# The token sums of a seven-product MLP block on VectorE instead of GpSimd

## What is computed

```python
h = _rmsnorm(x, g_pre_mlp)
f = jnp.square(jax.nn.relu(h @ w_up)) @ w_down
return x + _rmsnorm(f, g_post_mlp)
```

## Time and profile before

| | |
|---|---|
| time, median of 3 runs | 1090.42 us (1085.86 to 1091.12) |
| profiled execution | 1090.3 us |
| its span in the trace | 1088.7 us, 20822 instructions |
| mean granted clock of TensorE | 0.991 |
| busy: TensorE | 1051.5 us (97%) |
| busy: VectorE, ScalarE, GpSimd | 638.2, 482.1, 231.9 us |

### The profile page before, as it was taken

How to read it: one execution, slowest core, us unless ns; L and a number is a source line. 1 busy time by engine, 2 the same in 40 slices (tenths; PEclk the granted TensorE clock), 3 DMA queues, 4 the chain that set the end, 5 groups by cost and what they waited for, 6 DMA issues and landing times.

```text
span 1088.7 us, 20822 instructions
## 1 busy us (share of the span) xinstructions
PE 1051.5 (97%) x7528; PEld 896.3 (82%) x7528; DVE 638.2 (59%) x1229; ACT 482.1 (44%) x1026; POOL 231.9 (21%) x290
## 2 busy tenths in 40 slices
PE   7999999999999999999999999999899999999997
PEld 6987877887778777777779987998699889889985
DVE  5244535444765665555554847349877458447756
ACT  5253223323554465555543446344246236424641
POOL 4003111321001023333332000106642034024200
PEclk9999999999999999999999999999899999999999
DMA  6522214234125789999965261122332333333322
GB/s 204 142 82 59 60 56 137 61 83 139 40 58 161 247 286 343 335 332 335 336 206 183 82 227 39 59 79 78 89 104 90 100 95 88 116 112 98 110 87 87
DMA packets 114416, 153.16 MB, mean 141 GB/s; under 512 B 9597, under 2 KB 66434, under 8 KB 114322
## 3 DMA queue, kind: packets, MB, share of 16 engines
q1 hardware_dynamic: 99808, 106.98, 32.1%
q0 software_dynamic: 13120, 44.08, 12.2%
q10 hardware_dynamic: 1394, 0.83, 0.3%
HBM read 144.76 MB, written 7.10 MB: 139 GB/s over the span
## 4 chain that ended last, share of the span: by engine, by line
PE 82%; DVE 7%; DMA 3%; issue 3%; ACT 2%; SPq 1%; POOLq 1%; POOL 0%; DVEq 0%; ACTq 0%
PE ps L475 29%; PE ps L2661 12%; PE ps L910 7%; PE ps L510 7%; PE ps L483 5%; PE ps L1944 4%; PE ps L926 3%; PE ps L448 2%; DMA kring<-in_cache_k_dram 2%; PE ps L1953 2%; PE ps L1985 2%; PE ps L1074 1%; DVE xn L565 1%; PE ps L1094 1%; PE ps L1969 1%
## 5 line engine op out<-in xcount | busy, mean ns | idle before, releaser
L360 DVE TENSOR_TENSOR w<-w,w 128x512 fp32r<-128x512 f32 (+1 forms) x192 | 154.9, 818 | 159.0 <-ACT w L349 153.8
L349 ACT ACTIVATE w<-w 128x512 fp32r<-128x512 f32 (+1 forms) x192 | 115.1, 609 | 209.5 <-PE ps L483 148.4
L475 PE MATMUL ps<-w,hid 128*128 128x512 f32 x672 | 163.9, 393 | 5.0 <-DVE wide L2904 5.0
L475 PEld LDWEIGHTS ps<-w,hid 128*128 128x128 f32 x672 | 127.5, 190 | 32.0 <-issue 5.4
L475 PE MATMUL ps<-w,hT 128*128 128x512 f32 x576 | 146.1, 403 | 1.9 <-ACT ri L831 1.9
L475 PEld LDWEIGHTS ps<-w,hT 128*128 128x128 f32 x576 | 106.5, 191 | 27.1 <-issue 5.3
L910 PE MATMUL ps<-hT,w 128*128 128x288 f32 x768 | 126.8, 307 | 0.0
L910 PEld LDWEIGHTS ps<-hT,w 128*128 128x128 f32 x768 | 105.0, 188 | 12.3 <-issue 11.6
L1911 POOL DMA_DIRECT2D vring<-in_cache_v_dram x128 | 69.1, 539 | 172.2 <-issue 172.2
L2115 DVE COPY kT<-ps 128x512 f32<-128x512 f32 x64 | 44.1, 689 | 74.8 <-PE ps L1944 74.6
L1944 PEld LDWEIGHTS ps<-ident,kring 128*128 128x128 f32 x512 | 56.6, 141 | 37.5 <-DMA kring<-in_cache_k_dram 21.3
(11 more groups left out here) (403 smaller groups left out, 1811.2 us busy)
## 6 DMA issues: line engine op xcount, KB each, us to landing
kring<-in_cache_k_dram SPq DMA_DIRECT2D x128, 256.0 KB, 4.1
vring<-in_cache_v_dram POOLq DMA_DIRECT2D x128, 256.0 KB, 4.5
w<-in_w_in_dram SPq DMA_DIRECT2D x88, 256.0 KB, 2.9
w<-in_w_down_dram SPq DMA_DIRECT2D x64, 256.0 KB, 2.9
w<-in_w_up_dram SPq DMA_DIRECT2D x40, 256.0 KB, 2.9
b<-in_w_up_dram SPq DMA_DIRECT2D x36, 256.0 KB, 4.0
w<-in_w_out_dram SPq DMA_DIRECT2D x16, 256.0 KB, 3.2
x<-in_x_prompt_dram SPq DMA_DIRECT2D x4, 512.0 KB, 6.8
```

The lines of the kernel that those rows point to most:

```text
L349: eng.activation(spread(w_hi, n, j, width), together(w32, n, j, width), ACT.Copy)\
L360: eng.tensor_tensor(spread(w_lo, n, j, width), together(w32, n, j, width), spread(w_hi, n, j, width).bitcast(F32), ALU.subtract).then_inc( ...
L475: mm = eng.matmul(ps[:, t, :], left[a][:, k, prompt_cols(t)], w[b][:, j, :], start=(k == 0 and (a, b) == THREE[0]), stop=(k == kt - 1 and ...
```

## The change

The ten additions move from GpSimd's program into VectorE's. They and the four `token_low` are made one generator, `token_sums`, of fourteen pieces. VectorE takes two pieces behind each `w_low` of the first half of the first down projection from k = 1 on (and one behind each of the second half, should any be left). The order of the pieces is: sums 1 to 5, low part of S1, sums 6 and 7, low part of the second, sums 8 and 9, low part of the third, sum 10, low part of the fourth. ScalarE's `token_high` moves to the turns (0, 2), (0, 3), (0, 4), (0, 7). The low parts now count in `x_split`, in front of the weights' parts, and the weight sums in `w_sum`. GpSimd goes straight to `pool_sums`.

```diff
-    def pool_tokens(eng):
+    def token_sums(eng):
         eng.wait_ge(sem("hid_low"), 16)
-        eng.tensor_tensor(odd, A21[0], A22[0], ALU.subtract).then_inc(sem("t_sum"), 1)
+        eng.tensor_tensor(odd(), A21[0], A22[0], ALU.subtract).then_inc(sem("t_sum"), 1)
+        yield
         eng.wait_ge(sem("t_sum"), 1)
-        eng.tensor_tensor(odd, odd, A21[1], ALU.add).then_inc(sem("t_sum"), 1)
+        eng.tensor_tensor(odd(), odd(), A21[1], ALU.add).then_inc(sem("t_sum"), 1)
+        yield
...
+        token_low(eng, 0, odd())
+        yield
         eng.wait_ge(sem("t_sum"), 5)
-        eng.wait_ge(sem("t_low"), 1)
-        eng.tensor_tensor(odd, even, A12[0], ALU.add).then_inc(sem("t_sum"), 1)
+        eng.wait_ge(sem("x_split"), 1)
+        eng.tensor_tensor(odd(), even(), A12[0], ALU.add).then_inc(sem("t_sum"), 1)
+        yield
...
     def token_high(eng, m):
         eng.wait_ge(sem("t_sum"), (3, 5, 7, 10)[m])
...
-    def token_low(eng, m):
+    def token_low(eng, m, src):
         eng.wait_ge(sem("turned_high"), 4 * TILES + m + 1)
...
-    TOKEN_TURNS = ((0, 5), (0, 7), (1, 0), (1, 3))
+    TOKEN_TURNS = ((0, 2), (0, 3), (0, 4), (0, 7))
...
     def dve_mlp(eng, n):
+        tokens = token_sums(eng)
...
                     w_low(eng, n)
-                    if i == 0 and (c, k) in TOKEN_TURNS:
-                        token_low(eng, TOKEN_TURNS.index((c, k)))
+                    if i == 0 and (c, k) >= (0, 1):
+                        next(tokens, None)
+                        if c == 0:
+                            next(tokens, None)
...
             eng.memset(wide[:, :, :], 0.0).then_inc(sem("y_zero"), 1)
-            pool_tokens(eng)
             pool_sums(eng)
```

More of the change, by code:

```diff
@@ L2425, in moba_mlstm_step @@
     RING0 = 40
-    TSUMS = 10
+    TOKS_LOW = 4
     SLOT = {"P1": 4, "P6": 5, "P5": 6, "P2": 0, "P7": 1, "P4": 2, "P3": 3}
@@ L2467, in product_high @@
             else:
-                eng.wait_ge(sem("t_sum"), TSUMS + 2 * use + (1 if name == "P5" else 2))
+                eng.wait_ge(sem("w_sum"), 2 * use + (1 if name == "P5" else 2))
             if use:
@@ L2537, in sp_unit @@
             before = (i, j - 1) if j else (i - 1, UNITS - 1)
-            eng.wait_ge(sem("x_split"), extra_no("P1", *before) + 1)
-            eng.wait_ge(sem("t_sum"), TSUMS + 2 * v - 1)
+            eng.wait_ge(sem("x_split"), TOKS_LOW + extra_no("P1", *before) + 1)
+            eng.wait_ge(sem("w_sum"), 2 * v - 1)
             eng.dma_start(into(b11[:, :]), block(0, 0)).then_inc(sem("b_in"), 16)
@@ L2558, in half_of, with odd, even @@
         return h2T[part][:, 4 * kh:4 * kh + 4, h * HALFT:(h + 1) * HALFT]
-    def pool_tokens(eng):
+    def odd():
+        return rl[:, 0:4, :]
+    def even():
+        return rl[:, 4:8, :]
+    def token_sums(eng):
         A11, A12, A21, A22 = ([half_of(kh, h, part).bitcast(F32) for part in range(2)]
                               for h, kh in ((0, 0), (0, 1), (1, 0), (1, 1)))
-        odd, even = rl[:, 0:4, :], rl[:, 4:8, :]
         eng.wait_ge(sem("hid_low"), 16)
-        eng.tensor_tensor(odd, A21[0], A22[0], ALU.subtract).then_inc(sem("t_sum"), 1)
+        eng.tensor_tensor(odd(), A21[0], A22[0], ALU.subtract).then_inc(sem("t_sum"), 1)
+        yield
@@ L2567, in pool_tokens @@
         eng.wait_ge(sem("t_sum"), 1)
-        eng.tensor_tensor(odd, odd, A21[1], ALU.add).then_inc(sem("t_sum"), 1)
+        eng.tensor_tensor(odd(), odd(), A21[1], ALU.add).then_inc(sem("t_sum"), 1)
+        yield
         eng.wait_ge(sem("t_sum"), 2)
-        eng.tensor_tensor(odd, odd, A22[1], ALU.subtract).then_inc(sem("t_sum"), 1)
+        eng.tensor_tensor(odd(), odd(), A22[1], ALU.subtract).then_inc(sem("t_sum"), 1)
+        yield
         eng.wait_ge(sem("t_sum"), 3)
-        eng.tensor_tensor(even, odd, A11[0], ALU.subtract).then_inc(sem("t_sum"), 1)
+        eng.tensor_tensor(even(), odd(), A11[0], ALU.subtract).then_inc(sem("t_sum"), 1)
@@ L2573, in pool_tokens @@
+        yield
         eng.wait_ge(sem("t_sum"), 4)
-        eng.tensor_tensor(even, even, A11[1], ALU.subtract).then_inc(sem("t_sum"), 1)
+        eng.tensor_tensor(even(), even(), A11[1], ALU.subtract).then_inc(sem("t_sum"), 1)
+        yield
+        token_low(eng, 0, odd())
+        yield
         eng.wait_ge(sem("t_sum"), 5)
-        eng.wait_ge(sem("t_low"), 1)
-        eng.tensor_tensor(odd, even, A12[0], ALU.add).then_inc(sem("t_sum"), 1)
+        eng.wait_ge(sem("x_split"), 1)
+        eng.tensor_tensor(odd(), even(), A12[0], ALU.add).then_inc(sem("t_sum"), 1)
@@ L2578, in pool_tokens @@
+        yield
         eng.wait_ge(sem("t_sum"), 6)
-        eng.tensor_tensor(odd, odd, A12[1], ALU.add).then_inc(sem("t_sum"), 1)
-        eng.wait_ge(sem("t_low"), 2)
-        eng.tensor_tensor(even, A11[0], A21[0], ALU.subtract).then_inc(sem("t_sum"), 1)
+        eng.tensor_tensor(odd(), odd(), A12[1], ALU.add).then_inc(sem("t_sum"), 1)
+        yield
+        token_low(eng, 1, even())
+        yield
+        eng.wait_ge(sem("x_split"), 2)
+        eng.tensor_tensor(even(), A11[0], A21[0], ALU.subtract).then_inc(sem("t_sum"), 1)
@@ L2582, in pool_tokens @@
+        yield
         eng.wait_ge(sem("t_sum"), 8)
-        eng.tensor_tensor(even, even, A11[1], ALU.add).then_inc(sem("t_sum"), 1)
+        eng.tensor_tensor(even(), even(), A11[1], ALU.add).then_inc(sem("t_sum"), 1)
+        yield
+        token_low(eng, 2, odd())
+        yield
         eng.wait_ge(sem("t_sum"), 9)
-        eng.tensor_tensor(even, even, A21[1], ALU.subtract).then_inc(sem("t_sum"), 1)
+        eng.tensor_tensor(even(), even(), A21[1], ALU.subtract).then_inc(sem("t_sum"), 1)
@@ L2587, in moba_mlstm_step @@
+        yield
+        token_low(eng, 3, even())
     TOKS = (0, 1, 3, 2)
@@ L2590, in token_high @@
         eng.wait_ge(sem("t_sum"), (3, 5, 7, 10)[m])
-        eng.activation(tok[TOKS[m]][0], rl[:, 4 * (m % 2):4 * (m % 2) + 4, :], ACT.Copy)\
-           .then_inc(sem("turned_high"), 1)
-    def token_low(eng, m):
+        eng.activation(tok[TOKS[m]][0], odd() if m % 2 == 0 else even(), ACT.Copy).then_inc(sem("turned_high"), 1)
+    def token_low(eng, m, src):
         eng.wait_ge(sem("turned_high"), 4 * TILES + m + 1)
-        eng.tensor_tensor(tok[TOKS[m]][1], rl[:, 4 * (m % 2):4 * (m % 2) + 4, :], tok[TOKS[m]][0].bitcast(F32),
-                          ALU.subtract).then_inc(sem("t_low"), 1)
+        eng.tensor_tensor(tok[TOKS[m]][1], src, tok[TOKS[m]][0].bitcast(F32), ALU.subtract).then_inc(sem("x_split"), 1)
     def pool_sums(eng):
@@ L2604, in pool_sums @@
                 if v:
[L2605 to L2608, removed]
+                    eng.wait_ge(sem("x_split"), TOKS_LOW + 3 * v)
+                eng.tensor_tensor(t1s[:, :], b11[:, :], b12[:, :], ALU.add).then_inc(sem("w_sum"), 1)
+                eng.wait_ge(sem("w_sum"), 2 * v + 1)
+                eng.tensor_tensor(t2s[:, :], t1s[:, :], b22[:, :], ALU.add).then_inc(sem("w_sum"), 1)
                 eng.wait_ge(sem("w_split1"), use_of("P7", i, j))
                 eng.tensor_tensor(w32[:, 1, :], b12[:, :], b22[:, :], ALU.add).then_inc(sem("w_in1"), 16)
-                eng.wait_ge(sem("t_sum"), TSUMS + 2 * v + 2)
+                eng.wait_ge(sem("w_sum"), 2 * v + 2)
                 eng.wait_ge(sem("w_split2"), use_of("P4", i, j))
@@ L2649, in pe_units @@
         if i == 1:
-            eng.wait_ge(sem("t_low"), 4)
+            eng.wait_ge(sem("x_split"), 4)
         def product(name, j, bank, left, first):
@@ L2654, in product @@
             if name in EXTRA:
-                eng.wait_ge(sem("x_split"), extra_no(name, i, j) + 1)
+                eng.wait_ge(sem("x_split"), TOKS_LOW + extra_no(name, i, j) + 1)
             else:
```

## The result

| | before | after |
|---|---|---|
| median | 1089.93 us (22 runs, 1085.86 to 1093.38) | 1092.68 us (22 runs, 1088.58 to 1097.63) |
| profiled execution, its span | 1090.3 us, 1088.7 us | 1091.97 us, 1090.4 us |
| mean granted clock of TensorE | 0.991 | 0.992 |
| ratio to before | | 1.0032, 95% interval 1.0020 to 1.0043 |

The account below looks back on a forecast made before the run. The prediction took TensorE to bound the kernel, with one stop at VectorE's first drain. A drain 2.8 us later plus 0.1 us for the clock gave +2.9 us on 1090.3: 1093.2 us, range 1087.5 to 1097.0.

Parts of the forecast that it names:

- What bounds: TensorE bounds the kernel; its stop at the first down projection's PSUM drain costs 7.3 us, slow clock included.
- (2): All fourteen token pieces stand ahead of VectorE's first drain, taken at 1.27 us each, at most 1.5.
- (3): Four VectorE instructions directly needing the one before start 0.11 us after it, costing 0.19 us each, 0.76 in all.
- (4): Weight copies queue behind ScalarE's token copies; VectorE waits 4.1 us, drains at 768.90, and TensorE's stop is 7.8 us.
- (5): TensorE's clock falls during the stop either way; the longer stop adds 0.1 us of loss.
- the step behind it takes 5.2 us: Sign to look for: TensorE's weight step right behind the stop at the first drain takes 5.2 us.
- (6): Behind the drains, the seven products' blocks and GpSimd's first sum come 1.3 us later; these edits cost nothing.
- Rival 1: ScalarE waits and dependences are covered; stop of 3.0 us, 1088.3 us or, with the clock up, 1086.0; chance 0.15.
- Rival 2: The clock needs longer after the longer stop: 2.3 us more, together +5.2, 1095.6 us; chance 0.15.
- Rival 3: VectorE reaches the drain within 1 us of before, finding ScalarE's copies earlier; 1090.3 us within 1; chance 0.13.

Follow-up runs that it names:

- e1_spread: The changed kernel with eight of the fourteen token pieces in the first half and six in the second; ratio to the kernel before 0.9944.
- e5_small_sums: The kernel before with its ten GpSimd token sums cut to 8 of 1152 elements per partition; ratio to the kernel before 0.9942.
- e2: The changed kernel with ScalarE's first three token copies one weight step later; ratio to the kernel before 1.0000.
- e3_fillers: The changed kernel with 60 useless transposes on TensorE between the halves of the first down projection; ratio to the kernel before 1.0007.
- e4_after_again: The changed kernel, unaltered, run and profiled a second time; ratio to the kernel before 1.0020.

## Why the prediction was right

Right in sign and size: +2.9 us against +3.5 (2.2 to 4.7), with the mechanism forecast. The VectorE part of it was read and worked out; that the total came out so close owes something to luck, by the clock term below. By its steps:

- *What bounds.* The one stop at the first drain is where the change acts; nothing behind it gave or took time in the pair of profiles. e1_spread and e5_small_sums bound what was to be had there at 6 to 7.5 us (6.0 and 7.5 by the stages, 6.1 and 6.3 by the ratios), where the working from the earlier trace rows said 7.3.
- *(2) A sum on VectorE.* Bounded by the token low half (1.35 us, 1.27 to the next): measured 1.35.
- *(3) Dependences.* Sized too high. The second sum starts 0.03 us behind the end of the first (742.59 + 1.35, 743.97), not 0.11, so four cost 0.45 us and not 0.76.
- *(4) ScalarE's queue.* Forecast as gaps of 0.4, 0.6, 1.8 and 1.3 us, measured 0.36, 0.49, 1.75 and 1.23. e2 took the first three away and TensorE's stop fell by 2.9 us. The sum for VectorE was 27.5 us, measured 27.3; the drain was forecast at 768.90 and started at 768.64, the stop at 7.8 us and was 7.55.
- *(5) The clock.* The mean was about right, the reasoning was not. The prediction weighed two readings, a loss that grows with the stop and one stretch of about 4 us at half clock behind each restart, and neither is what the rows show. Around the earlier stop of the kernel before (the stop of 2.55 us ahead of 679.09):

```profile
679.00:680.00 1.00, 0.91 (x6) 0.74 0.00 0
...
682.00:684.00 2.00, 2.00 (x13) 0.78 0.00 0
```

There the clock falls at 679.48 and is back at 682.88: 3.4 us at half speed, all of it behind the restart. At the first drain of before it is 6.8 us (764.84 to 771.64), of which 4.75 lie behind the restart, where the prediction had 4.5. The slow stretch is not tied to the restart: after a stop of 7.55 us the loss was 1.4 us in one execution and 2.4 in the next (4.32 and 5.32 less 2.88), and 2.5 after the shorter stop of e2_copies_later. The term of +0.1 is therefore -0.9 or +0.1, and one pair of profiles could have read as +1.7 or +2.7. The sign "the step behind it takes 5.2 us" failed in the first profile (4.32) and came true in the second (5.32).
- *(6) Later work.* GpSimd's first weight sum was forecast 1.3 us later; it moved from 777.84 to 779.12:

```profile
779.12 1.28 POOL L2626 TENSOR_TENSOR t1s<-b,b 128x512 f32<-128x512 f32 x1 [84.62 <-DMA b<-in_w_up_dram]
```

- *The rivals.* Rival 1 (waits covered, faster) did not occur, since the gap behind sum 7 is there; but e2_copies_later shows that it depends on one line, and with three of the four gaps gone fourteen pieces still leave a stop of 4.69 us. Its price was probably too high besides: with the clock up, TensorE would have met the second wait of e3_fillers (0.54 us), so by estimate 1.8 us and not 2.3 were to be had there. Rival 2 was to take over if the slow stretch is longer than 9 us. Such a stretch exists, 10.2 us in e4_after_again, but half of it lay inside the stop, and it cost 1.0 us more than the other and not 2.3. Rival 3 is outside the measured interval of 2.2 to 4.7 us, and its condition was not there: the gaps came as written and the drain started 2.57 us later than before.

What stays open: by stage lengths the kernel after is 1.7 and 2.7 us slower in its two profiles, while the ratios say 3.5 (2.2 to 4.7) and 2.2 (0.5 to 3.8). The two ratios agree, and the stage of 2.7 lies in both intervals; that of 1.7, which is the pair of profiles under "The result", lies below the first. The pair shows no second place where time is lost. With one profile of before, the spread of its own stop is not known.

## What to carry to other kernels

When one PSUM bank set serves two halves, count what stands ahead of the first drain in the draining engine's program, and price a moved piece by that, not by its total: the same ten sums on the same engine were worth 7.5 us of the stage or cost 2, by whether eight or fourteen pieces stood there. Where two engines alternate in fixed orders, write out the starts of both, since an instruction waiting for a result of the other engine holds its own engine's next copy too; moving three such copies by one turn was worth 2.9 us of the stop. And a resource conflict that is removed only pays if the work that moves does not take its place on the same path.

## What the runs showed of the hardware

- VectorE's 128x512 subtraction with both inputs in SBUF took 0.69 us alone and 2.7 us beside GpSimd's sums of 3.0 us; with most of GpSimd's sums cut to 0.2 us it took 0.69 again. One sum took 3.0 us on GpSimd and 1.35 on VectorE. That 30 us of GpSimd's work could stop TensorE for 5 us was only visible in the drain's wait.
- After TensorE stopped, the clock fell 2.4 us later in one execution of the kernel and 3.6 us later in another, and stayed at 1.2 GHz for 10.2 and 6.8 us. So the loss behind a stop of 7.55 us is uncertain by 1 us, and is not larger than behind one of 4.7 or 5.0.
- Sixty transposes without use, 0.112 us each, kept the granted clock at 1.00 through a stop that they filled but for 1.0 us. They won 0.9 to 1.9 us, and not the whole 1.3 to 2.3 of the slow step, since TensorE at full clock ran into VectorE's last drain.
